# Expert blocks of 96 token slots in place of 128, in a two-layer hybrid decoder on one core

## The reference

```
logits = h @ router_w                       # 256 x 8
vals, idx = top_k(logits, 2)                # each token takes two experts
gate = one_hot(idx) weighted by softmax(vals)
out = sum over e of gate[:, e] * ((silu(h @ w1[e]) * (h @ w3[e])) @ w2[e])
```

## Time and profile before

| what | value |
|---|---|
| median of 3 runs | 1679.96 us |
| the profiled execution: span from first to last instruction | 1679.4 us |
| expert stage | about 717 to 1672 us |
| TensorE (PE) busy | 1641.7 us, 98% of the span, 8916 matmuls |
| weight loads (PEld) busy | 1383.1 us, 82% |
| VectorE (DVE) busy | 1363.4 us, 81% |
| ScalarE (ACT) busy | 1064.2 us, 63% |
| mean granted TensorE clock | 0.993 |
| read from memory | 473.40 MB |

### The profile page before, as it was taken

One profiled execution on the slowest core, in us unless ns is written; L12 is line 12 of the kernel. 1 busy time (PEld: TensorE's weight loads), 2 busy tenths in 40 slices (PEclk: granted clock), 3 DMA queues, 4 the chain that ended last, 5 costly groups with the idle time before them and its releaser, 6 DMA issues.

```text
span 1679.4 us, 24200 instructions
## 1 busy us (share of the span) xinstructions
PE 1641.7 (98%) x8916; PEld 1383.1 (82%) x8916; DVE 1363.4 (81%) x1134; ACT 1064.2 (63%) x894; POOL 445.0 (26%) x541
## 2 busy tenths in 40 slices
PE   8999999999999999999999999999999999999998
PEld 5887888988989788878888888888888888888886
DVE  4899675455569976788888988888888988888888
ACT  4345456444455554577777777777777777777774
POOL 8966802999143441234000000000000000000200
PEclk9999999999999999999999999999999999999999
DMA  8453456555544455489999999999999999999994
GB/s 293 160 159 114 172 191 219 177 187 200 169 152 151 151 164 178 139 298 395 381 381 390 368 379 383 361 394 390 369 387 375 363 394 383 378 385 369 390 395 188
DMA packets 212460, 481.57 MB, mean 287 GB/s; under 512 B 7937, under 2 KB 32641, under 8 KB 212145
## 3 DMA queue, kind: packets, MB, share of 16 engines
q1 hardware_dynamic: 207456, 463.34, 76.8%
q0 software_dynamic: 4512, 16.78, 2.7%
q10 hardware_dynamic: 432, 0.65, 0.1%
HBM read 473.40 MB, written 7.34 MB: 286 GB/s over the span
## 4 chain that ended last, share of the span: by engine, by line
PE 64%; DVE 5%; ACT 1%; issue 1%; DVEq 0%; ACTq 0%
PE ps L655 20%; PE ps L657 20%; PE ps L656 20%; DVE w_lo L286 2%; PE ps L1330 1%; PE ps L1406 0%; DVE top L2192 0%; DVE keybias L2171 0%; PE ps L1283 0%; PE ps L891 0%; DVE uv L2151 0%; PE ps L701 0%; ACT w_hi L280 0%; PE ps L702 0%; PE ps L703 0%
## 5 line engine op out<-in xcount | busy, mean ns | idle before, releaser
L286 DVE TENSOR_TENSOR w_lo<-raw,w_hi 128x2048 fp32r<-128x2048 f32 (+1 forms) x433 | 1007.7, 2330 | 223.5 <-ACT w_hi L280 221.9
L280 ACT ACTIVATE w_hi<-raw 128x2048 fp32r<-128x2048 f32 (+1 forms) x433 | 830.0, 1918 | 413.7 <-PE ps L657 328.1
L655 PE MATMUL ps<-w_hi,xg_hi 128*128 128x512 f32 x896 | 354.5, 396 | 1.2 <-DVE w_lo L286 1.2
L657 PE MATMUL ps<-w_hi,xg_lo 128*128 128x512 f32 x896 | 349.5, 390 | 0.0
L656 PE MATMUL ps<-w_lo,xg_hi 128*128 128x512 f32 x896 | 349.0, 389 | 0.0
L655 PE MATMUL ps<-w_hi,hidT_hi 128*128 128x512 f32 x520 | 203.7, 392 | 5.3 <-DVE hidT_lo L2460 5.3
L657 PE MATMUL ps<-w_hi,hidT_lo 128*128 128x512 f32 x520 | 202.4, 389 | 0.0
L656 PE MATMUL ps<-w_lo,hidT_hi 128*128 128x512 f32 x520 | 202.4, 389 | 0.0
L657 PEld LDWEIGHTS ps<-w_hi,xg_lo 128*128 128x128 f32 x896 | 168.2, 188 | 35.9
L655 PEld LDWEIGHTS ps<-w_hi,xg_hi 128*128 128x128 f32 x896 | 168.3, 188 | 35.4 <-DVE w_lo L286 1.7
L656 PEld LDWEIGHTS ps<-w_lo,xg_hi 128*128 128x128 f32 x896 | 168.4, 188 | 33.4
(11 more groups left out here) (432 smaller groups left out, 2407.4 us busy)
## 6 DMA issues: line engine op xcount, KB each, us to landing
raw<-moe_w SPq DMA_DIRECT2D x336, 1024.0 KB, 7.0
raw<-w_in SPq DMA_DIRECT2D x44, 1024.0 KB, 5.5
raw<-ffn_w SPq DMA_DIRECT2D x33, 1024.0 KB, 5.4
raw<-w_o SPq DMA_DIRECT2D x8, 1024.0 KB, 5.0
raw<-w_out_a SPq DMA_DIRECT2D x4, 1024.0 KB, 5.0
raw<-w_out_c SPq DMA_DIRECT2D x4, 1024.0 KB, 5.1
raw<-w_out_b SPq DMA_DIRECT2D x4, 1024.0 KB, 5.1
raw<-w_in SPq DMA_DIRECT2D x4, 904.0 KB, 9.3
```

The lines of the kernel that those rows point to most:

```text
L280: act.activation(w_hi[:, n % SPLIT, 0:width], raw[:, n % RAW, 0:width], ACT.Copy)\
L286: dve.tensor_tensor(w_lo[:, n % SPLIT, 0:width], raw[:, n % RAW, 0:width], w_hi[:, n % SPLIT, 0:width].bitcast(F32), ALU.subtract)\
L655: pe.matmul(dst, x_hi, hi, start=first, stop=False, skip_group_check=True)
L657: return pe.matmul(dst, x_lo, hi, start=False, stop=last, skip_group_check=True)
```

## The change

`SLOTS` becomes 96, and the round table gives each round its first slot and its width. Every stationary block of tokens, its copies, products and stores are cut to `width` partitions or columns. Tokens past 96 take two further rounds of 80 slots in the branch that held one of 128. Semaphore counts that depended on the round are generalised. Cut to its core:

```diff
-SLOTS = P
+SLOTS = 96
+ROUNDS = ((0, 96), (96, 80), (176, 80))
@@ counts
-            return 1 + 2 * BLOCKS if rnd == 0 else ACC_FIRST + 4 * e
+            return 1 + 2 * BLOCKS if rnd == 0 else ACC_FIRST + 4 * (EXPERTS * (rnd - 1) + e)
+        def scattered_before(rnd, e):
+            return 0 if rnd == 0 else 1 + EXPERTS * (rnd - 1) + e
@@ views used by ScalarE and VectorE
+        def quarters(t):
+            return t.rearrange("p (k n) -> p k n", k=4)
+        def eighths(t):
+            return t.rearrange("p (k n) -> p k n", k=KD)
@@ TensorE: rows (down), up, turn_hidden
-                    mm = three(ps[:, bank + 2 * b + h, :], x_hi[:, k0 + k, tok], x_lo[:, k0 + k, tok], n,
+                    mm = three(ps[0:tokens, bank + 2 * b + h, :], x_hi[:, k0 + k, tok], x_lo[:, k0 + k, tok], n,
-                            mm = three(ps[:, which, :], xg_hi[:, kk, :], xg_lo[:, kk, :], m,
+                            mm = three(ps[0:width, which, :], xg_hi[:, kk, 0:width], xg_lo[:, kk, 0:width], m,
-                        tr = pe.transpose(ps[:, 4, k * P:k * P + P], hid[:, k * P:k * P + P], ident[:, :])
+                        tr = pe.transpose(ps[:, 4, k * P:k * P + width], hid[0:width, k * P:k * P + P],
+                                          ident[0:width, 0:width])
@@ TensorE: first gather, find_tokens, turn_gathered
-                                mm = pe.matmul(ps[:, bank + k // 4, (k % 4) * P:(k % 4) * P + P],
-                                               src[:, b, k * P:k * P + P], pick[:, b, :],
+                                mm = pe.matmul(ps[:, bank + k // 4, (k % 4) * P:(k % 4) * P + width],
+                                               src[:, b, k * P:k * P + P], pick[:, b, 0:width],
-                        mm = pe.matmul(ps[:, 5, 0:1], pick[:, b, :].bitcast(F32), token_id[:, b:b + 1], start=b == 0,
+                        mm = pe.matmul(ps[0:width, 5, 0:1], pick[:, b, 0:width].bitcast(F32), token_id[:, b:b + 1], start=b == 0,
-                        tr = pe.transpose(ps[:, 6 + k // 4, (k % 4) * P:(k % 4) * P + P],
-                                          xg_tok[:, k * P:k * P + P], ident[:, :])
+                        tr = pe.transpose(ps[:, 6 + k // 4, (k % 4) * P:(k % 4) * P + width],
+                                          xg_tok[0:width, k * P:k * P + P], ident[0:width, 0:width])
@@ ScalarE
-                act.activation(dst, ps[:, bank, :], ACT.Copy).then_inc(S["hidT_hi_done"], 1)
+                act.activation(dst[:, :, 0:tokens], quarters(ps[:, bank, :])[:, :, 0:tokens], ACT.Copy)\
+                   .then_inc(S["hidT_hi_done"], 1)
@@ VectorE
-                    dve.tensor_scalar(pick[:, b, :], slot_id[:, rnd, :], slot_of[:, b, bass.ds(e, 1)], None,
+                    dve.tensor_scalar(pick[:, b, 0:width], flat(slot_id[:, :, :])[:, first:first + width], slot_of[:, b, bass.ds(e, 1)], None,
-                dve.tensor_tensor(dst, ps[:, bank, :], hi.bitcast(F32), ALU.subtract)\
+                dve.tensor_tensor(dst[:, :, 0:tokens], quarters(ps[:, bank, :])[:, :, 0:tokens],
+                                  hi[:, :, 0:tokens].bitcast(F32), ALU.subtract).then_inc(S["hidT_lo_done"], 1)
@@ GpSimd
-                pool.dma_start(y_rows[e * P:(e + 1) * P, :], y_sb[:, :]).then_inc(S["rows_stored"], 16)
+                pool.dma_start(y_rows[e * SLOTS:(e + 1) * SLOTS, :], y_sb[0:SLOTS, :]).then_inc(S["rows_stored"], 16)
-                pool.indirect_dma_start(xg_tok[:, :], None, h_rows, bass.IndirectOffsetOnAxis(token_of[:, 0:1], 0))\
+                pool.indirect_dma_start(xg_tok[0:SLOTS, :], None, h_rows,
+                                        bass.IndirectOffsetOnAxis(token_of[0:SLOTS, 0:1], 0))\
@@ the branch, on each engine
             with pe.If(most_tokens > SLOTS):
                 experts(1)
+                experts(2)
```

More of the change, by code:

```diff
@@ L1337, in down @@
                         rows(n + half, 2 * half, xT_hi, xT_lo, first and half == 0, False, bank=2, blocks=1,
-                             seen=n + half + 1 + 6 * turns, middle=middle if half == 0 else None)
+                             seen=n + half + 1 + 6 * turns, middle=middle if half == 0 else None, tokens=width)
                 def last_down(n, i, turns):
@@ L1344, in last_down @@
                         cols = slice(half * HALF, (half + 1) * HALF)
-                        dst = ps[:, 2 + half, :]
+                        dst = ps[0:width, 2 + half, :]
                         for chunk in range(2):
@@ L1353, in last_down @@
                             for k in range(2):
[L1354 removed]
+                                pe.matmul(dst, xg_hi[:, 2 * chunk + k, 0:width], hi[:, k, cols], start=False, stop=False,
                                           skip_group_check=True)
[L1356 removed]
+                                pe.matmul(dst, xg_lo[:, 2 * chunk + k, 0:width], hi[:, k, cols], start=False, stop=False,
                                           skip_group_check=True)
@@ L1360, in last_down @@
                             for k in range(2):
-                                mm = pe.matmul(dst, xg_hi[:, 2 * chunk + k, :], lo[:, k, cols], start=False, stop=False,
+                                mm = pe.matmul(dst, xg_hi[:, 2 * chunk + k, 0:width], lo[:, k, cols], start=False, stop=False,
                                                skip_group_check=True)
@@ L1413, in turn_pick @@
                     for b in range(BLOCKS):
-                        tr = pe.transpose(ps[:, 5, b * P:b * P + P], pick[:, b, :].bitcast(F32), ident[:, :])
+                        tr = pe.transpose(ps[0:width, 5, b * P:b * P + P], pick[:, b, 0:width].bitcast(F32), ident[:, :])
                     tr.then_inc(S["pickT_ps"], 1)
                 def scatter(e, last):
-                    scattered = 0 if rnd == 0 else 1 + e
+                    scattered = scattered_before(rnd, e)
                     pe.wait_ge(S["pickT_done"], scattered + 1)
@@ L1947, in experts @@
                 i0 = DENSE_STRIPES + e0 * MOE_STRIPES
+                width = ROUNDS[rnd][1]
                 def xg(e, turned):
                     act.wait_ge(S["gather_ps"], 2 * (e0 + e) + (2 if turned else 1))
-                    act.activation(flat(xg_hi[:, :, :]), banks(6 if turned else 4, 2), ACT.Copy)\
+                    act.activation(xg_hi[:, :, 0:width], eighths(banks(6 if turned else 4, 2))[:, :, 0:width], ACT.Copy)\
                        .then_inc(S["xg_hi_done"], 1)
@@ L1959, in stripe @@
                     split_hi(act, n0 + 8, turns)
-                    hidden_hi(i + t - 1, 4)
-                    silu(i + t, n0 + 6 + 6 * turns)
+                    hidden_hi(i + t - 1, 4, width)
+                    silu(i + t, n0 + 6 + 6 * turns, rows=width)
                     split_hi(act, n0 + 9, turns)
@@ L2018, in experts @@
                     choice_exp()
-                silu(i0, n0 + 2)
+                silu(i0, n0 + 2, rows=width)
                 split_hi(act, n0 + 4)
@@ L2436, in mixer, with times_up @@
                 chunk(34)
-            def times_up(sil_seen, w3_used, turned, width=HALF, lows=None):
+            def times_up(sil_seen, w3_used, turned, width=HALF, lows=None, rows=P):
                 dve.wait_ge(S["sil_done"], sil_seen)
@@ L2622, in stripe @@
                     lo(n0 + 8, turns)
-                    hidden_lo(prev, 4)
+                    hidden_lo(prev, 4, width)
                     lo(n0 + 9, turns)
-                    times_up(this, w3_at, turned)
+                    times_up(this, w3_at, turned, rows=width)
                 def y(e, y_used=None, halves=(0, 1)):
@@ L2732, in experts @@
                 times_up(i0 + 1, n0 + 4, i0 - DENSE_STRIPES if rnd else None,
-                         lows=None if rnd else DENSE_STRIPES)
+                         lows=None if rnd else DENSE_STRIPES, rows=width)
                 lo(n0 + 5, 0)
```

72 lines of the change are left out of this document (37 added, 35 removed).

## The result

The changed kernel takes 1687.45 us, median of 12 runs (1686.22 to 1688.56); the kernel before, timed beside it, 1683.88 us, median of 12 (1679.73 to 1685.59). The ratio is 1.0026, 95% interval [1.0018, 1.0034]. Forecast were 1671.5 us in a range of 1664 to 1680. So 0.3% slower, in place of 0.5% faster.

A forecast was written before the change was run, and what follows sets the result against it. TensorE's own sequence was taken to bound the expert stage. Gains of 6.0 + 1.5 + 0.75 + 0.2 = 8.4 us off the 1679.4 us span gave 1671.0, with 0.6 between span and time 1671.5 us; range 1664 to 1680.

The forecast's parts named there:

- part 1: Stationary blocks of 96 columns in the 4,032 big matmuls: shorter loads hidden behind the matmul before, value 0, upper bound 53.6 us.
- rival B: The 13.3 ns bubble between big matmuls shrinks by a quarter: 13.4 us more gain, 1658.1 us (gone: 1618); chance 0.09.
- the sum: All gains together, 6.0 + 1.5 + 0.75 + 0.2 = 8.4 us, giving a span of 1671.0 and 1671.5 us.
- Parts 2 and 3: Transposes of hidden block and gathered tokens, 6.0 and 1.5 us gained; token lookup's shorter loads, 0.75 us gained.
- The last transpose's share: First matmul after the transposes waits for last stream and own load; both shrink by 27 ns, so this gain counts.
- Rival A: The 128-column load is the floor of a transpose, so most transpose gain falls away: gain 2.6, 1677.3 us; chance 0.22.
- Part 4: Start of the expert stage: first gather's loads gain 0; smaller picks and second low copy gain together 0.2 us.
- Part 5: VectorE and ScalarE work, views, row gathers, stores, weight DMAs and the overflow branch cost nothing; no wait is added.
- Rival C: Each change between 96-column blocks and 128-column transposes drains the array, 0.19 us: +24 us against -8.4, 1695.5 us; chance 0.07.

## Why the prediction was wrong, point by point

**The step that failed** is in part 1: "That is 26 ns off a load that is already 30 ns early. Value: 0", and "Lower bound 0, as nothing gets longer". The load did shrink by 27 ns and was early before and after; the settled distance between matmuls grew by 3.33 ns all the same, 10.9 us for the eight experts. I reasoned as if load and stream only met at the end of the load. The runs show that they settle into a common pattern which depends on the block's width and on its place beside the moving columns. With full blocks put back the period fell from 119.34 to 118.13; narrow blocks alone raised it from 119.00 to 120.37. The trace of before had no fp32r row under 128 columns, and I had said so against rival B ("no row has fewer than 128 columns in this format"); the bound should have been open on both sides, and the 3.3 ns that rival B gave, taken as a loss, would have made 1671.5 + 13.4 = 1684.9.

Of the 15.95 us between forecast and result, 11.3 are the periods (8 x (119.34 - 117.93)). Another 3.9 are the base: three runs of the kernel before had the median 1679.96, twelve have 1683.88. The last 0.7 are not assigned. The 0.6 us that the sum put between span and time is too small as well: the recorded runs have about 1.7 (1687.40 beside a span of 1685.7).

**Rival B** had the right size and place with the wrong sign: 3.3 ns a pair, lost and not won. The size is luck, since the loss does not go by the columns left out (97 and 88 columns cost nothing in the bare stream, 120 cost 6.7 ns). Its sentence that from 2 ns a pair this outweighs everything was the one to follow. With 256 moving columns the sign would have been right, 120.0 to 116.1, but not the rule by quarters: 112 columns have 113.3.

**Parts 2 and 3** were right: transposes 109 to 82 ns, four in 0.33, eight in 0.66; lookup 0.11 less in all (0.34 + 0.34 to 0.26 + 0.31). The last transpose's share, which part 2 counted as real, shows at the second matmul behind the turn (0.316 to 0.288 us) and needs the narrow blocks too: with full blocks it stays at 0.316. Rival A (the load as floor) is wrong; with 80 columns a transpose takes 69.

**Part 4**: the first gather to the first big matmul went from 3.73 us (713.01 to 716.74) to 3.61 (717.24 to 720.85), 0.1 for the 0.2 forecast.

**Part 5** held: TensorE 100% busy, weight chunks 336, landing in 6.9 us, the branch not run.

**The sum, again**, for one period: 119.00; turns and lookup with the second matmul behind each turn -1.02 (forecast -1.07); big matmuls +1.38 where the runs have settled and -0.02 where they have not. That makes 119.34, as measured. The forecast's error is the +1.36 that it had at 0.

**Rival C** was wrong: no drain of 0.19 us shows (0.28 us to the second matmul behind a turn, 0.32 before). The Trainium skill's list of column modes (128, 64 and 32; "TensorEngine Tiling (Array Packing)", section "Available Configurations", not "Key Properties" as the prediction has it), by which 96 columns stay in the full mode, agrees with that. The figure of the Trainium skill for a pair of load and matmul at 512 columns, about 131 ns ("TensorE: Matmul & The Clock Gate", section "Back-to-back issue gap"), does not agree with the runs: at granted clock 1.00 the least of all fp32r streams here was 226.7 ns, of bf16 215.8.

**Open**: why place and width matter. That the reads of the two operands get in each other's way in memory, where the pattern repeats with 64 columns, is a guess; no run separates this from other causes. Nor is it settled what in the kernel picks the pattern at a turn.

## What to carry to other kernels

An operand that is smaller, and a load that is shorter, can make a tight stream slower; where a stream of load and matmul pairs is the bound, measure the distance between starts at the new shape in a bare stream before counting on zero, and in the kernel too, as the bare stream misses patterns that a run can fall into. Change one side of a tuned pair at a time: the cheap part of this change (fewer columns in transposes and lookups) was worth 0.3% with 96 slots and 0.5% with 80 once the stationary blocks of the big matmuls kept their width and alignment. Read such distances from starts over many instructions, since 3 ns disappear in a chain that rounds to 0.23, and look at the first ten of a run apart, since here they hide a fifth of the difference.

## What the hardware showed unexpectedly

Stationary blocks in fp32r with 512 moving columns: 226.7 to 237.0 ns between matmuls, by width and by the block's first column against the moving one's, in the main repeating with 64 columns; full blocks moved by 8 columns lose 3% (226.7 to 233.3). The same stream in bf16 stays at 215.8 at 128, 112, 96 and 80 columns. A pattern, once settled within some ten matmuls, lasted for the whole run of 72, and two of them (227 and 233) occurred at one shape in one kernel, by turns.
